# Prompt attention's values two tiles behind their scores, and each projection tile in one piece

## The reference, cut to what matters

```
h = rms_norm(x, norm_mix)
q, k, v, u, ga, gp = split(h @ w_in)            # q, k normalised per 64-wide component
for each block of 128 queries:                  # causal
    s = (q @ k.T) * 64 ** -0.5                  # both components
    s = where(kpos <= qpos, s, -1e30)
    p = softmax(s)[component 0] - lam * softmax(s)[component 1]
    o = p @ v                                   # 128 queries x 128
```

## Time and profile before

| what | value |
|---|---|
| median of three runs | 2158.81 us (2157.7 to 2162.5) |
| profiled execution, its own time | 2162.38 us |
| its span, first to last instruction | 2160.6 us |
| mean granted TensorE clock | 0.994 of full speed |
| PE busy | 2096.9 us, 97% |
| DVE, ACT, POOL busy | 49%, 31%, 23% |
| loop over the heads, on TensorE | 67.1 to 572.0 us of the span |

### The profile page before, as it was taken

How to read it: one execution, slowest core, us unless ns; L and a number is a source line. 1 busy time by engine, 2 the same in 40 slices (tenths; PEclk the granted TensorE clock), 3 DMA queues, 4 the chain that set the end, 5 groups by cost and what they waited for, 6 DMA issues and landing times.

```text
span 2160.6 us, 34490 instructions
## 1 busy us (share of the span) xinstructions
PE 2096.9 (97%) x13501; PEld 1907.2 (88%) x13501; DVE 1067.6 (49%) x1389; ACT 671.2 (31%) x1322; POOL 503.2 (23%) x382
## 2 busy tenths in 40 slices
PE   6999999999999999999999999999999999999998
PEld 6788888888888887899999887999999899999996
DVE  5566667666310101266773433555555555555555
ACT  4344454444443333224112311311221122122120
POOL 5423333332010101332331100311221221122120
PEclk9999999999999999999999999999999999999999
DMA  5222111222367886211124420201110111111112
GB/s 154 58 56 58 40 55 34 56 60 75 126 225 269 285 279 221 84 50 55 59 78 130 123 88 1 70 20 60 50 40 30 54 55 41 31 49 60 31 39 94
DMA packets 174539, 186.00 MB, mean 86 GB/s; under 512 B 8239, under 2 KB 147259, under 8 KB 174402
## 3 DMA queue, kind: packets, MB, share of 16 engines
q1 hardware_dynamic: 163786, 175.21, 26.0%
q10 hardware_dynamic: 10624, 8.92, 1.2%
HBM read 161.09 MB, written 23.24 MB: 85 GB/s over the span
## 4 chain that ended last, share of the span: by engine, by line
PE 85%; issue 6%; DVE 3%; POOL 2%; DMA 1%; ACT 1%; SPq 0%; ACTq 0%; POOLq 0%; DVEq 0%
PE PS L1362 33%; PE PS L2017 12%; PE PS L913 8%; PE PS L279 4%; PE PS L281 4%; PE PS L280 4%; PE PS L1839 4%; PE PS L313 3%; PE PS L337 3%; PE PS L968 3%; PE PS L326 2%; PE PS L983 2%; PE PS L1022 1%; POOL fw_lo L1349 1%; PE PS L292 1%
## 5 line engine op out<-in xcount | busy, mean ns | idle before, releaser
L1349 POOL TENSOR_TENSOR fw_lo<-fw_raw,fw_hi 128x1024 fp32r<-128x1024 f32 x86 | 215.7, 2508 | 883.0 <-ACT fw_hi L1345 838.4
L1362 PE MATMUL PS<-m_hi,fw_hi 128*128 128x384 f32 (+1 forms) x1032 | 228.4, 329 | 3.1 <-issue 1.8
L1362 PE MATMUL PS<-m_lo,fw_hi 128*128 128x384 f32 (+1 forms) x1032 | 227.4, 328 | 0.0
L1362 PE MATMUL PS<-m_hi,fw_lo 128*128 128x384 f32 (+1 forms) x1032 | 227.4, 328 | 0.0
L2144 DVE TENSOR_TENSOR x<-x,PS 128x512 f32<-128x512 f32 x198 | 135.9, 688 | 141.0 <-PE PS L2017 140.9
L279 PE MATMUL PS<-w_hi,act_hi 128*128 128x384 f32 (+1 forms) x520 | 188.2, 362 | 0.0
L1362 PEld LDWEIGHTS PS<-m_hi,fw_hi 128*128 128x128 f32 x1032 | 175.8, 188 | 4.1 <-issue 2.4
L281 PE MATMUL PS<-w_hi,act_lo 128*128 128x384 f32 (+1 forms) x520 | 176.7, 340 | 0.0
L1362 PEld LDWEIGHTS PS<-m_hi,fw_lo 128*128 128x128 f32 x1032 | 176.3, 188 | 0.0
L1362 PEld LDWEIGHTS PS<-m_lo,fw_hi 128*128 128x128 f32 x1032 | 176.2, 188 | 0.0
L280 PE MATMUL PS<-w_lo,act_hi 128*128 128x384 f32 (+1 forms) x520 | 176.1, 339 | 0.0
(11 more groups left out here) (261 smaller groups left out, 4288.5 us busy)
## 6 DMA issues: line engine op xcount, KB each, us to landing
k_pg<-in_cache_k_dram SPq DMA_DIRECT2D x64, 512.0 KB, 4.8
v_pg<-in_cache_v_dram SPq DMA_DIRECT2D x64, 512.0 KB, 5.2
fw_raw<-in_w_up_dram SPq DMA_DIRECT2D x44, 512.0 KB, 4.1
fw_raw<-in_w_in_dram SPq DMA_DIRECT2D x24, 512.0 KB, 4.8
wd_raw<-in_w_down_dram SPq DMA_DIRECT2D x22, 512.0 KB, 4.1
w_raw<-in_w_in_dram SPq DMA_DIRECT2D x21, 512.0 KB, 5.3
out_dram<-raw SPq DMA_DIRECT2D x16, 512.0 KB, 3.7
ga_scratch<-ga_ring ACTq DMA_DIRECT2D x8, 544.0 KB, 7.1
```

The source lines that it names most:

```text
L1349: e.tensor_tensor(fw_lo[slot][:, 0:kts, :], fw_raw[:, 0:kts, :], fw_hi[slot][:, 0:kts, :].bitcast(F32), ALU.subtract).then_inc(fw_tail, 1)
L1362: ins = e.matmul(PS[:, 3 * slot + c, 0:cw], w[slot][:, kt, :], x[:, kt, c0:c0 + cw], start=first and kt == 0, stop=last and kt == KT - 1)
```

## The change

The score of step s stays two steps ahead of the values now instead of one. TensorE's order in a head becomes: scores of 0 and of 1 back to back (in different pairs of banks, `scores_of`), two whole projection tiles, and then for s = 2 to 7: transposes of the probabilities of s-2, at most one group of q or k transposes, scores of s, values of s-2, one whole projection tile. The tail has the probabilities of 6, the ninth tile with values 6 and the probabilities of 7 in its middle, and values 7. The second group of transposed probabilities goes to the free projection bank or, for the last two, to a score bank. Bank 7 is divided: columns 0 to 383 for q and k, 384 to 511 for the result, each with semaphores of its own.

VectorE's queue keeps its order. On ScalarE a step is now: copies of the transposed probabilities of s-2, copy of q or k, copy of the result of s-2, exponentials of s, a weight piece, copy of the projected tile. The three weight pieces stand at s = 0, 1 and 3, behind the exponentials. On GpSimd they stand at the same s, where they are ahead of the gain (s = 1) and of the inverse root (s = 3). In head 6 the two pieces of the gate weights stay at s = 0 and 3, of which the second comes ahead of the inverse root too.

```diff
         def pe_head(e, h, slot, proj):
-            for s in range(TT):
-                if s < QT:
-                    pe_scores(e, h, slot, s)
...
-                if s == QT:
-                    matmuls({3: q_and_first, 5: k_and_second})
-                elif s < 5:
-                    matmuls({2: first_and_q, 5: k_part})
                 else:
-                    first_group()
-                    q_part()
-                    matmuls({2: second_group, 5: k_part})
-                if s >= 1:
-                    pe_values(e, h, slot, s - 1, b_use(h, proj, ("o", s)))
...
+            for s in range(2):
+                pe_scores(e, h, slot, s)
+            for s in range(2):
+                project(s)
+            for s in range(2, QT):
+                probs(s - 2, s)
+                pe_scores(e, h, slot, s)
+                pe_values(e, h, slot, proj, s - 2)
+                project(s)
+            probs(QT - 2, QT)
+            project(QT, {4: last_two})
+            pe_values(e, h, slot, proj, QT - 1)
...
         def act_head(e, h, slot, proj, split, stored):
...
+            for s in range(QT):
+                if s >= 2:
+                    probs(s - 2, s)
+                    values(s - 2)
+                act_exp(e, h, s)
+                if s == 0 and proj:
+                    e.wait_ge(pj_full, h * TT + TT)
+                if split and s in (0, 1, 3):
+                    act_split_w(e, h + 2, slot, (0, 1, 3).index(s))
+                elif proj and not split and s in (0, 3):
+                    fm_head(e, s // 3, s // 3)
+                take_matmuls(s)
...
         def pool_head(e, step, h, slot, proj, split):
             for s in range(TT):
                 if s == 0:
                     pool_rstd_qk(e, step, h, 2)
-                    if split:
-                        pool_split_w(e, h + 2, slot, 0)
-                    elif proj:
-                        fm_tail(e, 0, 0)
+                if split and s in (0, 1, 3):
+                    pool_split_w(e, h + 2, slot, (0, 1, 3).index(s))
+                elif proj and not split and s in (0, 3):
+                    fm_tail(e, s // 3, s // 3)
                 if s == 1:
                     pool_gain_qk(e, h, slot, 2)
                 if proj and s in (4, 7):
                     pool_gain_qk(e, h + 1, 1 - slot, s // 3 - 1)
                 if proj and s in (3, 6):
                     pool_rstd_qk(e, step, h + 1, s // 3 - 1)
-                    if split:
-                        pool_split_w(e, h + 2, slot, s // 3)
-                    elif s == 3:
-                        fm_tail(e, 1, 1)
```

More of the change, by code:

```diff
@@ L282, in pe_project, with pe_qk_transposes, scores_of @@
             ins.then_inc(pj_full, 1)
[L284 to L303, removed]
+        def pe_qk_transposes(e, n, slot, g, part, use, values):
+            if part == 0:
+                e.wait_ge(gained_qk, n * 3 + g + 1)
+            e.wait_ge(qk_free, use)
+            if not isinstance(values, int) or values:
+                e.wait_ge(o_free, values)
+            for j in range(3):
+                t = 3 * g + j
+                ins = e.transpose(PS[:, B_O, j * P:j * P + rows(t)],
+                                  raw[slot][0:rows(t), t, part * VD:(part + 1) * VD],
+                                  ident[0:rows(t), 0:rows(t)])
+            ins.then_inc(qk_full, 1)
+        def scores_of(s):
+            n = (s + 1) * P
+            if s < 2:
+                return PS[:, 2 * s:2 * s + 2, 0:n]
+            return scores_ps[:, :, 0:n]
         def pe_scores(e, h, slot, s):
-            if s == 0:
-                e.wait_ge(b7_free, FIRST_USES - 1 + h * USES_PER)
-            e.wait_ge(exp_done, h * QT + s + 1)
+            if s % 3 == 0:
+                e.wait_ge(qk_free, QK_FIRST - 2 + h * QK_PER + 2 * (s // 3))
+            if s != 1:
+                e.wait_ge(exp_done, h * QT + s + 1)
             n = (s + 1) * P
@@ new lines, in project, with probs @@
+            def project(s, between={}):
+                if proj:
+                    pe_project(e, h + 1, 1 - slot, s, between)
+                else:
+                    pe_chunk(e, s, between)
+            def probs(s, place):
+                pe_probs_transpose(e, h, slot, s, 0)
+                if s >= 4:
+                    pe_probs_transpose(e, h, slot, s, 1)
+                part = qk_part(h, slot, proj, place)
+                if part:
+                    pe_qk_transposes(e, *part, h * QT + s)
@@ L401, in pe_phase1 @@
                 if s in (5, 8):
-                    pe_qk_transposes(e, 0, 0, s // 3 - 1, 2 * (s // 3 - 1))
+                    for part in range(2):
+                        pe_qk_transposes(e, 0, 0, s // 3 - 1, part, 2 * (s // 3 - 1) + part, 0)
             with e.Fori(0, NH // 2 - 1) as i:
@@ L448, in act_evac_probs @@
             w = min(4, s + 1 - 4 * g) * P
[L449 removed]
+            bank = probs_tail_bank(slot, s) if g else B_PT
+            e.activation(PTs[(PT_AT[s] + g) % 2][:, 0:w], PS[:, bank, 0:w], ACT.Copy).then_inc(pt_free, 1)
         def act_exp(e, h, s):
@@ new lines, in probs, with values @@
+            def probs(s, place):
+                act_evac_probs(e, h, slot, s, 0)
+                if s >= 4:
+                    act_evac_probs(e, h, slot, s, 1)
+                part = qk_part(h, slot, proj, place)
+                if part:
+                    act_evac_qk(e, *part)
+            def values(s):
+                if s == 0:
+                    e.wait_ge(o_st[1], h * 16 + 1)
+                if s == QT // 2:
+                    e.wait_ge(o_st[0], h * 16 + 16)
+                e.wait_ge(o_full, h * QT + s + 1)
+                e.activation(osb[:, s % (QT // 2), :], PS[:, B_O, O_AT:O_AT + VD], ACT.Copy).then_inc(o_free, 1)
+                if s % (QT // 2) == QT // 2 - 1:
+                    half = s // (QT // 2)
+                    e.wait_ge(o_free, h * QT + s + 1)
@@ L507, in act_sumsq_x @@
+            probs(QT - 2, QT)
+            values(QT - 2)
+            probs(QT - 1, QT + 1)
+            take_matmuls(QT)
+            values(QT - 1)
         def act_sumsq_x(e, t):
@@ L536, in act_phase1 @@
                 if t == 6:
-                    act_evac_qk(e, 0, 0, 0, 0)
+                    for part in range(2):
+                        act_evac_qk(e, 0, 0, 0, part, part)
             act_evac_projection(e, 0, 0, TT - 1, 0)
-            act_evac_qk(e, 0, 0, 1, 2)
+            for part in range(2):
+                act_evac_qk(e, 0, 0, 1, part, 2 + part)
             e.wait_ge(lam_step, 1)
```

174 lines of the change are left out of this document (57 added, 117 removed).

## The result

The changed kernel takes 2168.3 us (median of 8, 2166.3 to 2168.9), the kernel before 2159.2 beside it on the same chip (8 runs, 2156.9 to 2166.3): ratio 1.003, 95% interval 1.0019 to 1.0042. It is slower, by about 9 us; forecast were 8.9 us and 2167.7. The profiled execution is 2168.94 (span 2167.0), at the upper end of its runs.

A forecast was written before the change was run, and what follows sets the result against it. TensorE was taken as the bound, busy 62.19 of 62.74 us in a steady head. Heads 1 to 5 +1.86 each (+9.3), head 0 +0.1, head 6 about 0, head 7 -0.5: +8.9 on 2158.81, so 2167.7; range 2146 to 2178.

The forecast's parts named there:

- scores 3: Start of step 3's scores after the head's first score: 18.6 us against 18.14 before, TensorE waiting about 2.6.
- rest of the head: From step 3's scores to the head's end: 44.6 us as before, plus 1.05 and 0.65, minus 0.3.
- the clock: TensorE's clock in steady heads 1 to 5: no fall forecast, so no term in the +1.86 us.
- The turns: VectorE and GpSimd alternate by instruction: scaling about 3.5 us, division of step 1 some 2.7, piece 1 about 3.6.
- rival B: No change: VectorE gets two more small operations in ahead of the gain; +0.4 us a head, 2159 in all; chance 0.16.
- The further waits: Late gain for step 5's transposes and late copies of q for step 1's values: about 0.65 us, bounds 0 and 1.84.
- The moved work and the smaller savings: After step 3's scores: moved values and raw transposes add 1.05 us, smaller savings take off 0.3.
- rival C: Slower still: the clock falls in every head behind a two-part wait, 1.7 us each, +8.5, 2176; chance 0.12.
- Head 0: Step 3's scores at 21.1 us; head shorter by 2.4, plus 2.5 for a clock fall: +0.1.
- Heads 6 and 7: Head 6 about 0, its second gate piece ahead of the inverse root; head 7, without projection or piece, -0.5 us.
- The pair of scores: Scores of steps 0 and 1 together save one entry and one exit: 0.4 us a head, bounds 0 and 0.42.
- Rival A: Faster: VectorE keeps its turn through several instructions, TensorE is never held; heads of 61.5 us, median 2144; chance 0.22.

The follow-up runs named there:

- after: The changed kernel itself, 2168.3 us, ratio 1.003 to the kernel before; profiled twice, the second execution's own time being 2169.39.
- Smaller piece 1: Changed kernel with weight piece 1 cut to 384 of 1152 columns, its rest moved to piece 2: 2169.3 us, ratio 1.0047.
- wait filled: Changed kernel with ten thrown-away matmuls ahead of the scores of step 3 in heads 0 to 6: 2171.0 us, ratio 1.005.
- root first: Changed kernel with weight pieces back at steps 0, 3 and 6 and GpSimd's inverse root ahead of the piece: 2148.8 us, ratio 0.9948.
- gain first: Changed kernel with GpSimd's gain on q and k at step 1 ahead of weight piece 1: 2169.8 us, ratio 1.0043.

## Why the prediction was right

The size, the sign and the mechanism came out; the terms below the sum less well, and that they add up so closely is luck. Take the second execution of after, in which every steady head is alike:

| step, a steady head | forecast | measured | read from |
|---|---|---|---|
| scores 3 | 18.6 (+0.46) | 17.5 to 17.65 (-0.5) | TensorE, head 4; wait 1.90 instead of 2.6 |
| rest of the head | +1.4 | +1.2 | head 3 of after: 63.29 - 17.51 = 45.78, before 44.6 |
| the clock | 0 | +1.2 | 64.5 without the fill, 63.3 with it |
| sum | +1.86 | +1.8 to +1.9 | |

**The turns: right.** Three rows forecast at 3.5, 2.7 and 3.6 us (scaling, division, piece 1) took 3.43, 2.55 and, with piece 0, 6.01 together, which is 3.35 if piece 0 took its 2.66. The earlier trace rows had shown it for another pair of loops. "Smaller piece 1" shows that it is the cause: with a piece shorter by 1.75 us (two thirds of 2.64) scores 3 came forward by 1.65 to 1.7 in every head from 0 to 5 that has the wait.

**Scores 3 at 18.6: mis-sized by 1.0 to 1.1.** The step that failed is "gets its turn to 13.3; POOL's gain (1.82) runs to 15.1; DVE's last two operations of these probabilities take 0.64". Piece 1 ended at 12.65 after the head's first score instead of 12.9, and the gain did not wait for the division: it ran from 12.6 to 14.5. Of the last two operations, the tiny one (L589) ran beside it, and the other ended 0.28 behind it. So the probabilities were out at 14.8 instead of 15.8, and from there to scores 3 it took 2.86 us, for 2.84. TensorE reached the transposes at about the same time, so the wait had one part and not two. This is near to rival B, which let two small operations in ahead of the gain: one got through, but beside it.

**The rest of the head: +1.2 for +1.4, by other terms.** The further waits, set at 0.65, did not come: head 4 is idle for 1.90 us in all, which is the one wait for the exponentials. The moved work and the smaller savings, set at +0.75 together, came to +1.2; no run parts them.

**The clock: rival C's mechanism, at 0.12, was real.** The forecast's range for a head contained its cost, but not by a term of its own. In one execution of after every head 0 to 5 had a fall of 3.41 us behind the wait. In the other one heads 1, 4 and 5 did, head 3 did not, and head 2's came with the stop for instructions. Each fall of 3.41 us costs 1.2 us ("wait filled"; head 3 against head 4 gives 1.27), not the 1.7 of C. The argument against C, a stretch of phase 3 with 5.41 of 9.50 us busy at full clock, was taken from too different a place. So the sum of a head was right by luck: scores 3 set 1.0 too late and a rest of the head 0.2 too long stood for a fall that was left out. In heads 1 to 5 it is +9.5 for +9.3.

**Head 0.** Forecast +0.1, measured -1.3 and -2.3 in two executions. Scores 3 moved from 24.9 to 20.2, by 0.9 more than the forecast 21.1; the clock fell at their side for 6.83 us in one execution and for 3.41 in the other, where before it fell ahead of them. The rest of the head took 47.9 and 47.0 us where 48.5 were set (46.0 and 2.5 for the clock): that term was too high, within its bounds.

**Heads 6 and 7.** -0.5 and -0.4, for about 0 and -0.5.

**The whole: 9.0 for 8.9 is closer than the parts.** In the second execution of after, heads 1 to 5 are 9.5 us longer, head 0 is 2.3 and heads 6 and 7 are 0.9 shorter, so that the loop is 6.3 longer, for a forecast 8.9. The profiled executions' own times say the same: 2168.94 and 2169.39, where 2171.3 was forecast from the own time before. It is the medians, 2159.2 and 2168.3, that differ by 9.0; beside the later experiments the kernel before had 2161.1 and 2162.1.

**The pair of scores: right.** In head 4, counted from start to start and without the matmuls of the projection (0.17 each), the scores of steps 0 and 1 cost 0.53 and 0.82 us before, and 0.97 together after: 0.38 less, for 0.4. In head 3 of after, without a fall, TensorE is busy 61.29 us against 62.19 in head 4 before; what makes up the other 0.5 of this 0.9 no run parts.

**Rival A** failed as a forecast and is the most useful of them: its 61.5 a head is what TensorE needs when nothing shuts out DVE, and "root first" reached 61.3 to 61.5. The change contains two things, a better order of TensorE with what goes with it, worth 1.25 us a head, and pieces moved to where DVE needs the shared path, worth 1.93 of wait and 1.2 of clock. The second alone costs the kernel before some 30 us (2191.2 against 2161.1).

**Open.** What makes the clock fall behind one wait of 1.9 us and not behind the same wait in head 3, nor behind one of 1.94 in head 5 of "gain first" (63.5 us long); and what brings the stop for instructions, which was there in 4 of the 9 profiles of versions and in one of two of after itself, each time where the loop jumps back, in front of head 2 or of head 4. The stop is not what makes after slow: its two profiles differ in it and end within 0.5 us of each other (own times 2168.94 and 2169.39), since the one with the stop has a head without a fall and a tail shorter by 1.8 us.

## What to carry to other kernels

When work is moved on GpSimd, ask which of VectorE's operations it will shut out and what waits for these, not only what is queued behind it: here a piece of 2.66 us, on an engine that is busy a quarter of the time, made TensorE wait 1.9 us in each head. If a change of order loses, time its parts apart: the gain of one (-0.5% when cleaned up) was hidden under the loss of the other. And a wait that a trace shows can have a second price in TensorE's clock, which was found here by comparing equal heads with and without a fall.

## What the runs showed of the hardware

- VectorE and GpSimd took turns, instruction by instruction, where both wanted the shared path: VectorE 3.43 for 0.95 behind one piece, then 2.55 for about 0.4 behind the next, then 1.82 for 0.48 beside the gain. The Trainium skill ("SBUF — State Buffer", "Who interferes with whom") says of the modes of VectorE that use two ports that whoever issues first has the shared pair for the whole instruction and the other is blocked; the lengths in the trace agree, though it does not show the modes, and it adds who comes next when both wait.
- Not every small operation was held. One on one column (L589) took its usual 0.20 beside the gain in after and beside piece 1 in "gain first"; the scaling of two columns took 2.60 beside piece 0 in the kernel before, for 0.17 elsewhere.
- A wait of 1.9 us, behind 0.7 us of transposes and a shorter gap, was followed by 3.41 us at 1.2 GHz instead of 2.4 in all five steady heads of one execution and in three of the four with this wait in the other, and behind 1.9 us in four of five in "gain first". It cost 1.2 us, and with matmuls whose result is thrown away in the wait it did not come in heads 1, 2, 3 and 5.
- TensorE stopped for 2.1 to 3.2 us between two heads in four profiles, in after some 4 us behind two instruction packets of 16 KB on queue 8, and in one execution of the same kernel but not in the other. All four stops stand where the loop over pairs of heads jumps back. The profiles without one have no packet on queue 8 from 200 to 430 us; those with one have some behind it, six from 205 to 430 us in after. That this is a fetch of TensorE's instructions is inferred.
